# Nine full pieces of a head's probability blocks instead of twelve mixed ones

## The reference

```python
SEQ, MLA_HEADS, QK_HEAD, V_HEAD, Q_BLOCK = 1024, 16, 96, 64, 128
...
    def block(i):
        start = i * Q_BLOCK
        qb = lax.dynamic_slice_in_dim(q, start, Q_BLOCK, axis=1)
        s = jnp.einsum('bqhd,bkhd->bhqk', qb, k,
                       preferred_element_type=jnp.float32) * scale
        q_idx = start + jnp.arange(Q_BLOCK)
        s = jnp.where(k_idx[None, :] <= q_idx[:, None], s, -jnp.inf)
        p = jax.nn.softmax(s, axis=-1)
        return jnp.einsum('bhqk,bkhd->bqhd', p.astype(v.dtype), v)
...
    o = causal_attention(q, k, v)
    return x + (o * jax.nn.silu(z)) @ w_out
```

## Time and profile before

| what | us |
| --- | --- |
| median of three runs | 961.99 (960.85 to 962.02) |
| span of the profiled execution | 960.9 |
| TensorE matmul busy | 947.5 |
| VectorE busy | 812.9 |
| ScalarE busy | 575.2 |
| GpSimd busy | 353.1 |

### The profile page before, as it was taken

The page is one execution under the profiler, slowest core; times in us unless marked ns, Lnnn a source line. Parts: engine busy times, 40 slices in busy tenths (PEclk is TensorE's granted clock), DMA queues, the critical chain, the costliest instruction groups (busy, mean ns, idle before and its releaser), DMA issues.

```text
span 960.9 us, 17257 instructions
## 1 busy us (share of the span) xinstructions
PE 947.5 (99%) x6406; PEld 671.3 (70%) x6406; DVE 812.9 (85%) x1410; ACT 575.2 (60%) x1076; POOL 353.1 (37%) x393
## 2 busy tenths in 40 slices
PE   9999999999999999999999999998999999999998
PEld 8788544444688887644457999996788888887443
DVE  5798899899865579988887899998999999998763
ACT  6443544424434454454646888866899989997230
POOL 0002233222000002235412577875652478894220
PEclk9999999999999999999999999999999999999999
DMA  9320422111054422332123264566676775460231
GB/s 305 45 61 23 110 77 56 44 45 45 1 175 155 152 67 67 107 112 58 31 72 111 89 205 150 204 181 176 119 163 145 171 150 122 82 179 2 88 110 65
DMA packets 165347, 103.74 MB, mean 108 GB/s; under 512 B 75272, under 2 KB 149520, under 8 KB 165008
## 3 DMA queue, kind: packets, MB, share of 16 engines
q1 hardware_dynamic: 159216, 102.25, 38.0%
q10 hardware_dynamic: 6048, 0.39, 0.5%
HBM read 56.48 MB, written 29.36 MB: 89 GB/s over the span
## 4 chain that ended last, share of the span: by engine, by line
PE 72%; DVE 19%; POOL 3%; issue 3%; ACT 2%; DVEq 0%; POOLq 0%; ACTq 0%
PE banks L111 19%; PE banks L113 19%; PE banks L112 19%; PE banks L2728 7%; PE banks L2746 2%; PE banks L2748 2%; PE banks L2747 2%; DVE heads_y L2480 1%; POOL heads_prod L2616 1%; DVE heads_x L2476 1%; DVE heads_x L2475 1%; DVE front_lt L1223 1%; DVE heads_ss L2522 1%; PE banks L2756 1%; DVE front_l L1223 1%
## 5 line engine op out<-in xcount | busy, mean ns | idle before, releaser
L2497 DVE TENSOR_TENSOR heads_pt_lo<-banks,heads_pt_hi 128x512 f16<-128x512 f32 (+2 forms) x192 | 102.1, 554 | 10.8 <-ACT heads_pt_hi L2360 7.8
L2360 ACT ACTIVATE heads_pt_hi<-banks 128x512 f16<-128x512 f32 (+2 forms) x192 | 89.1, 487 | 9.1 <-PE banks L2728 8.9
L2748 PE MATMUL banks<-heads_v,heads_pt_lo 128*128 128x64 f16 x576 | 71.1, 194 | 0.0
L2747 PE MATMUL banks<-heads_v,heads_pt_hi 128*128 128x64 f16 x576 | 71.0, 194 | 0.0
L2489 DVE CUSTOM_DVE_ANT_0 heads_probs_big<-banks,heads_mask,score_scale 128x1024 f32<-128x1024 f32 (+1 forms) x64 | 68.6, 1072 | 2.9 <-PE banks L113 2.7
L2746 PE MATMUL banks<-heads_v,heads_pt_hi 128*128 128x64 f16 x576 | 70.9, 194 | 0.0
L2728 PE MATMUL banks<-ident,heads_probs_big 128*128 128x128 f32 x416 | 69.5, 281 | 1.2 <-ACT heads_probs_big L2351 1.1
L2351 ACT ACTIVATE heads_probs_big<-heads_probs_big,heads_neg_max 128x1024 f32<-128x1024 f32 (+1 forms) x64 | 63.4, 990 | 8.8 <-DVE heads_neg_max L2489 7.7
L111 PE MATMUL banks<-heads_k_t,heads_q_t 96*128 96x512 f16 (+2 forms) x192 | 63.0, 328 | 1.0 <-DVE heads_neg_max L2489 1.0
L111 PE MATMUL banks<-front_act_hi,front_w_hi 128*128 128x512 f32 x160 | 63.8, 399 | 0.0
L113 PE MATMUL banks<-front_act_hi,front_w_lo 128*128 128x512 f32 x160 | 62.4, 390 | 0.0
(11 more groups left out here) (489 smaller groups left out, 3114.5 us busy)
## 6 DMA issues: line engine op xcount, KB each, us to landing
qk_scratch<-heads_y SPq DMA_DIRECT2D x22, 512.0 KB, 3.7
front_x<-in_x_t SPq DMA_DIRECT2D x16, 512.0 KB, 5.3
front_raw<-in_w_in_ab SPq DMA_DIRECT2D x14, 512.0 KB, 5.1
qk_scratch<-heads_last_y SPq DMA_DIRECT2D x10, 512.0 KB, 3.8
front_w<-in_w_out_ab SPq DMA_DIRECT2D x8, 512.0 KB, 3.9
x_scratch<-front_x SPq DMA_DIRECT2D x8, 512.0 KB, 3.9
v_scratch<-heads_v SPq DMA_DIRECT2D x32, 128.0 KB, 3.0
heads_v_st<-v_scratch SPq DMA_DIRECT2D x8, 512.0 KB, 5.2
```

The source lines that it names most:

```text
L2360: nc.scalar.activation(pt_hi[:, q % PIECES, :width], t_ps[:, banks[("piece", n, k)] % 3, :width], ACT.Copy).then_inc(pt_high, 1)
L2497: nc.vector.tensor_tensor(pt_lo[:, q % PIECES, :width], t_ps[:, banks[("piece", n, k)] % 3, :width], pt_hi[:, q % PIECES, :width], ALU.sub ...
L2747: nc.tensor.matmul(o_part, pt_hi[:, q % PIECES, blk], v2[e][:, j, VH:], start=False, stop=False)
L2748: last = nc.tensor.matmul(o_part, pt_lo[:, q % PIECES, blk], v2[e][:, j, :VH], start=False, stop=(j == i))
```

## The change

The order of row tiles becomes 7, 3, 6, 0, 5, 1, 4, 2: tiles 0 and 2 change places. The rest of a wide tile is no longer a piece of its own; it shares a piece and a bank with the narrow tile behind it: tile 6's last three blocks with tile 0's one, tile 5's last two with tile 1's two, tile 4's last one with tile 2's three. Tile 7 has two full pieces and tile 3 one. So each position has one piece of four blocks, the first has two, and a head has nine. `PIECES_OF` writes that out. `high` and `low` always work on four blocks. Reciprocals, row maxima and the outputs of a head are kept by position instead of by row tile, so that the groups of four are contiguous; the output turn looks the position up.

```diff
-ORDER = (7, 3, 6, 2, 5, 1, 4, 0)
+ORDER = (7, 3, 6, 0, 5, 1, 4, 2)
...
-    def pieces(i):
-
-        return [range(b, min(b + 4, i + 1)) for b in range(0, i + 1, 4)]
...
+    PIECES_OF = (((0, range(0, 4)), (0, range(4, 8))), ((1, range(0, 4)),), ((2, range(0, 4)),),
+                 ((2, range(4, 7)), (3, range(0, 1))), ((4, range(0, 4)),), ((4, range(4, 6)), (5, range(0, 2))),
+                 ((6, range(0, 4)),), ((6, range(4, 5)), (7, range(0, 3))))
+
+    def pieces(n):
+
+        p, base = n % NT, n // NT * NT
+        if p == 0:
+            return [[(base, j) for j in blocks] for _, blocks in PIECES_OF[0]]
+        return [[(base + tile, j) for tile, blocks in PIECES_OF[p] for j in blocks]]
...
+    def turned_by(n):
+
+        last = n + 1 if n % NT in (2, 4, 6) else n
+        return piece_no(last, len(pieces(last)) - 1) + 1
...
-            nc.scalar.activation(pt_hi[:, q % PIECES, :width], t_ps[:, banks[("piece", n, k)] % 3, :width],
+            nc.scalar.activation(pt_hi[:, q % PIECES], t_ps[:, banks[("piece", n, k)] % 3],
                                  ACT.Copy).then_inc(pt_high, 1)
...
-            act.wait_ge(pv_done, piece_no(4 * g + 3, len(pieces(ORDER[(4 * g + 3) % NT])) - 1) + 1)
+            act.wait_ge(pv_done, piece_no(4 * g + 3, 0) + 1)
...
-                dve.wait_ge(pt_ready, piece_no(n - 4, len(pieces(tile_of(n - 4)[1])) - 1) + 1)
+                dve.wait_ge(pt_ready, turned_by(n - 4))
...
-            nc.vector.tensor_tensor(pt_lo[:, q % PIECES, :width], t_ps[:, banks[("piece", n, k)] % 3, :width],
-                                    pt_hi[:, q % PIECES, :width], ALU.subtract).then_inc(pt_low, 1)
+            nc.vector.tensor_tensor(pt_lo[:, q % PIECES], t_ps[:, banks[("piece", n, k)] % 3],
+                                    pt_hi[:, q % PIECES], ALU.subtract).then_inc(pt_low, 1)
...
-            nc.gpsimd.tensor_tensor(
-                pair_tiles(pair, g, e), o_raw[:, g % 2].rearrange("p (a b) d -> p a b d", a=2),
-                group_tiles(inv[:, h % 2], g).unsqueeze(3).to_broadcast([P, 2, 2, VH]),
-                ALU.mult).then_inc(o_scaled, 1)
+            nc.gpsimd.tensor_tensor(pair_tiles(pair, g, e), o_raw[:, g % 2],
+                                    group_tiles(inv[:, h % 2], g).unsqueeze(2).to_broadcast([P, 4, VH]),
+                                    ALU.mult).then_inc(o_scaled, 1)
...
-            for r, j in enumerate(pieces(tile_of(n)[1])[k]):
-                last = nc.tensor.transpose(t_ps[:, b, r * P:(r + 1) * P], probs(n, j * P, (j + 1) * P), ident[:])
+            for r, (m, j) in enumerate(pieces(n)[k]):
+                last = nc.tensor.transpose(t_ps[:, b, r * P:(r + 1) * P], probs(m, j * P, (j + 1) * P), ident[:])
...
-            o_part = o_ps[:, g % 2, o_slot(i), :VH]
-            for r, j in enumerate(pieces(i)[k]):
-                blk = slice(r * P, (r + 1) * P)
+            for r, (m, j) in enumerate(pieces(n)[k]):
+                i, blk, o_part = tile_of(m)[1], slice(r * P, (r + 1) * P), o_ps[:, g % 2, m % 4, :VH]
...
-                last = nc.tensor.transpose(t_ps[:, b, r * P:(r + 1) * P], o_pair[:, pair % 2, 4 * c + r, :], ident[:])
+                last = nc.tensor.transpose(t_ps[:, b, r * P:(r + 1) * P],
+                                           o_pair[:, pair % 2, ORDER.index(4 * c + r), :], ident[:])
```

More of the change, by code:

```diff
@@ L2175, in tile_of @@
         return divmod(n, NT)[0], ORDER[n % NT]
-    def pieces(i):
-        return [range(b, min(b + 4, i + 1)) for b in range(0, i + 1, 4)]
-    PER_HEAD = sum(len(pieces(i)) for i in range(NT))
+    PIECES_OF = (((0, range(0, 4)), (0, range(4, 8))), ((1, range(0, 4)),), ((2, range(0, 4)),),
[6 more added lines that the diff above has]
+        return [[(base + tile, j) for tile, blocks in PIECES_OF[p] for j in blocks]]
+    PER_HEAD = sum(len(pieces(p)) for p in range(NT))
     def piece_no(n, k):
         h, p = divmod(n, NT)
-        return PER_HEAD * h + sum(len(pieces(ORDER[x])) for x in range(p)) + k
+        return PER_HEAD * h + sum(len(pieces(x)) for x in range(p)) + k
+    def turned_by(n):
+        last = n + 1 if n % NT in (2, 4, 6) else n
+        return piece_no(last, len(pieces(last)) - 1) + 1
     def turn_step(pair, c):
@@ L2194, in heads_and_attention @@
         if n < N:
-            for k in range(len(pieces(tile_of(n)[1]))):
+            for k in range(len(pieces(n))):
                 banks[n_banks] = (pt_low, piece_no(n, k) + 1)
@@ L2224, in group_tiles @@
     def group_tiles(tile, g):
-        half = 1 if g % 2 == 0 else 0
-        return tile.rearrange("p (a c b) -> p a c b", a=2, c=2)[:, :, half, :]
+        return tile[:, g % 2 * 4:g % 2 * 4 + 4]
     def pair_tiles(pair, g, e):
[L2230 to L2235, removed]
+        return o_pair[:, pair % 2, g % 2 * 4:g % 2 * 4 + 4, e * VH:(e + 1) * VH]
     def sync(sp):
@@ L2350, in exponentials @@
             act.wait_ge(s_free, n + 1)
-            nc.scalar.activation(row, row, ACT.Exp, bias=neg_max[:, h % 2, i:i + 1], scale=-1.0,
-                                 accum_out=total[:, h % 2, i:i + 1]).then_inc(exp_done, 1)
+            at = n % NT
+            nc.scalar.activation(row, row, ACT.Exp, bias=neg_max[:, h % 2, at:at + 1], scale=-1.0,
+                                 accum_out=total[:, h % 2, at:at + 1]).then_inc(exp_done, 1)
         def high(n, k):
-            width = len(pieces(tile_of(n)[1])[k]) * P
             q = piece_no(n, k)
@@ L2487, in maxima @@
             if n >= 4:
-                dve.wait_ge(pt_ready, piece_no(n - 4, len(pieces(tile_of(n - 4)[1])) - 1) + 1)
+                dve.wait_ge(pt_ready, turned_by(n - 4))
             nc.vector.tensor_tensor_reduce(probs(n, 0, width), scores(i, 0, width), mask[:, S - width:],
                                            score_scale[:], 3e38, ALU.add, ALU.min,
-                                           neg_max[:, h % 2, i:i + 1]).then_inc(s_free, 1)
+                                           neg_max[:, h % 2, n % NT:n % NT + 1]).then_inc(s_free, 1)
         def low(n, k):
-            width = len(pieces(tile_of(n)[1])[k]) * P
             q = piece_no(n, k)
             dve.wait_ge(pt_high, q + 1)
-            nc.vector.tensor_tensor(pt_lo[:, q % PIECES, :width], t_ps[:, banks[("piece", n, k)] % 3, :width],
-                                    pt_hi[:, q % PIECES, :width], ALU.subtract).then_inc(pt_low, 1)
+            nc.vector.tensor_tensor(pt_lo[:, q % PIECES], t_ps[:, banks[("piece", n, k)] % 3],
+                                    pt_hi[:, q % PIECES], ALU.subtract).then_inc(pt_low, 1)
         def inverse(g):
@@ L2726, in transposes @@
                 pe.wait_ge(exp_done, n + 1)
-            for r, j in enumerate(pieces(tile_of(n)[1])[k]):
-                last = nc.tensor.transpose(t_ps[:, b, r * P:(r + 1) * P], probs(n, j * P, (j + 1) * P), ident[:])
+            for r, (m, j) in enumerate(pieces(n)[k]):
+                last = nc.tensor.transpose(t_ps[:, b, r * P:(r + 1) * P], probs(m, j * P, (j + 1) * P), ident[:])
             last.then_inc(pt_ready, 1)
         def product(n, k):
-            h, i = tile_of(n)
-            e, g = h % 2, n // 4
+            e, g = n // NT % 2, n // 4
             q = piece_no(n, k)
             if n % NT == 0 and k == 0:
-                pe.wait_ge(v_low, h + 1)
+                pe.wait_ge(v_low, n // NT + 1)
             if n % 4 == 0 and k == 0:
@@ L2801, in tensor @@
             old = n - BEHIND
-            new_pieces = len(pieces(tile_of(n)[1])) if n < N else 0
-            old_pieces = len(pieces(tile_of(old)[1])) if 0 <= old < N else 0
+            new_pieces = len(pieces(n)) if n < N else 0
+            old_pieces = len(pieces(old)) if 0 <= old < N else 0
             if n == N:
```

## The result

| | before | after |
| --- | --- | --- |
| median of five runs, us | 961.92 (960.85 to 962.02) | 965.13 (964.62 to 965.59) |
| span of the profiled execution | 960.9 | 963.8 |

The ratio is 1.0033, with an interval of 1.0023 to 1.0044: slower by a third of a per cent. The forecast was 965.3.

What follows compares the result with a forecast made beforehand. TensorE bounds the steady heads before; afterwards a ScalarE-VectorE loop was to. Steady part +2.7 us, end +0.6, first head 0: +3.3 on the 960.9 span, 964.2, and 1.1 more for the median: 965.3 us, 8-in-10 range 961.2 to 968.0.

Steps and rivals of the forecast that it cites:

- The loop as summed: Four turns a head of maxima, exponentials, copy, subtraction between VectorE and ScalarE: 13.50 us, against TensorE's 13.10.
- the rival that VectorE's total is the bound: VectorE's total work, not TensorE, bounds the kernel; less of it saves 7.2 us, giving 954.8; chance 0.04.
- The steady part: From tile 8's maxima to tile 126's: 200.87 us before, 203.54 forecast, so +2.7 us.
- The end: After tile 126's maxima: plain output products start at +3.83 us instead of +3.41, last products +0.17; +0.6 us in all.
- the first head: Stretch up to tile 8, paced by the last projections and a low-clock stretch: taken as 0, bounds -0.5 and +0.4 us.
- the two positions named: Positions 2 and 4 of a head, where TensorE was to wait for exponentials and for maxima.
- the third rival: TensorE's new waits, up to 0.4 us each, bring more stretches at half clock: 970 us; chance 0.07.
- edits with one answer: Tile order, semaphore waits, GpSimd's multiply, DMAs and piece slots: each costs 0, hidden by TensorE or the loop.
- a microsecond to spare: Before the change the loop took 12.04 us a head and hid under TensorE's 13.10.
- no longer on the path: In heads with an output turn, TensorE's eight transposes of that turn, 0.87 us, were to stop setting the pace.
- The gating: Wait of an output turn taken into the loop: 0.57 us, once in each of seven heads, 3.99 us.

Runs made afterwards that it cites:

- run 5: Changed kernel; from the third head on, copy and subtraction of odd positions' pieces treat two of four blocks, the rest left out: 961.13 us, ratio 0.9994.
- run 6: Changed kernel; from the third head on, copy and subtraction of even positions' last pieces treat two of four blocks, the rest left out: 964.20 us, ratio 1.0026.
- run 9: Changed kernel with a VectorE reciprocal of four columns added behind each odd position's subtraction: 968.18 us, ratio 1.0064.
- run 10: Changed kernel with a VectorE reciprocal of four columns added behind each even position's subtraction: 965.67 us, ratio 1.0039.
- run 11: Kernel before with the new order of tiles and bookkeeping by position, but its twelve pieces a head: 965.88 us, ratio 1.0038.
- run 2: Changed kernel with only the reciprocal of four row sums moved behind the next wide tile's maxima: 965.19 us, ratio 1.0030.
- run 12: Changed kernel with tile 6's rest of three blocks given its own piece and bank again, ten pieces a head: 963.72 us, ratio 1.0017.
- run 8: Kernel before with copy and subtraction of the wide tiles' rests, at even positions, taking all 512 columns: 966.81 us, ratio 1.0048.
- run 7: Kernel before with copy and subtraction of the narrow tiles' pieces, at odd positions, taking all 512 columns: 970.21 us, ratio 1.0089.
- run 1: Changed kernel with VectorE issuing odd positions' subtractions and the reciprocal behind the next wide tile's maxima: 979.69 us, ratio 1.0184.
- run 3: Changed kernel with a 32-column VectorE copy added behind each odd position's subtraction: 988.18 us, ratio 1.0273.
- run 4: Changed kernel with a 32-column VectorE copy added behind each even position's subtraction: 974.97 us, ratio 1.0137.

## Why the prediction was right, and where it was not

**The bound after.** The loop as summed is there: 13.41 us a head against 13.50. Each turn was read 0.02 or 0.03 too long, above all from maxima to exponentials (1.16 and not 1.19 at 896 columns, 0.89 and not 0.91 at 640). With runs 5, 6, 9 and 10 the loop is shown to set the pace of the heads without a turn, and the rival that VectorE's total is the bound is shown false. The Trainium skill (Perfetto Trace Analysis, Identifying the Most-Contended Engine) says to optimize first the engine of highest occupancy. The runs differ from it here: run 6 leaves VectorE busy 22.20 of 27 us and takes 964.2, run 5 leaves it 23.07 and takes 961.1.

**The sum.** The steady part was forecast at 203.54 and took 203.50, by errors that cancel, which is luck: 14 heads and most of a last one at 0.09 less are 1.3 us; the turn costs a head 0.71 (14.12 less 13.41) and not 0.57, seven times 0.14, 1.0 more (six heads and the last one, not seven before it); and the first of the 14 heads takes 13.71, 0.3 more (13.69 before). The end was forecast at 3.83 and 0.17 of products, and took 3.85 and 0.19. The 0.33 by which tile 8 comes earlier is not the first head's: its first maxima already come 0.46 earlier (658.37 against 658.83; the profiled runs here lie between 657.86 and 659.72), and it takes 0.13 longer, inside the bounds of that term.

**The waits.** In a head without a turn TensorE's distances exceed the usual ones by 0.53 us in all, 0.22 before. Of the 0.31 more, position 2's first transposes have 0.26 and position 4's 0.10, the two positions named; the rest of the head has a little less than before. The granted clock was 1.00, the upper of its two levels, from 676 to 885 us, so the third rival didn't come.

**The step that failed** in the account of what the change costs stands among the "edits with one answer": the order of tiles, at 0, "hidden by TensorE or the loop". Run 11 puts the order alone at 3.9 us over the kernel before (965.88 against 962.02 on the same chip). The sum still came out because the two losses don't add: in the heads without a turn, where the whole loop already sets the pace, the narrower chain of run 11 lies beside it (13.41 with both, 13.25 with the order alone). So the forecast named rightly what bounds the changed kernel's heads without a turn, but "the full pieces cost 3 us" doesn't follow. With the new order they cost nothing that can be told, 1.0033 (1.0023 to 1.0044) with them and 1.0038 (1.0025 to 1.0050) without: their heads without a turn are 0.16 longer, and the early ones with a turn 0.54 shorter. The prediction looked at the loop as one sum over a head, with a microsecond to spare before. It didn't ask whether each part of a head has its share of that; there the room was 0.2 us.

A second step failed in the heads with a turn: TensorE's transposes of the turn were taken to be "no longer on the path". The rows and four runs say that they are. The gating costs the loop its 0.57, as summed, and the copy that waits for TensorE 0.15 more. With the loop shortened by runs 2 and 12 these heads stay at 14.12; with the loop lengthened (run 9) or that copy halved (run 6) the turn costs 0.60.

No kernel with the whole computation was faster than the one before. **What is open**: the excess of run 8, the early heads with a turn of run 11, and run 2's time.

## What to carry to other kernels

Follow a piece of work round all engines that wait for each other in their written order, and sum the turns: an instruction on that loop costs each time what it delays the next start, and the same instruction beside it nothing, as long as it doesn't come to stand ahead of one on the loop (run 7). Make that sum for each part of a period too, against the work that covers it there, because moving cover from one position to another costs as much as lengthening the loop. Moving an instruction behind another one's wait closes a new loop (run 1), so name what stands in front of it before it moves.

## What the runs showed of the hardware that was not expected

A small copy on VectorE can last as long as the instruction that GpSimd is running. In run 3 the 34 copies that began with GpSimd idle took 172 ns in the median and 175 at most; the 30 that began while it was busy took 562 in the median and up to 2108. In run 4 it was 172 and 174 against 475 and 1651. The reciprocal of four columns, put in the same places in runs 9 and 10, kept a mean of 167 and 168 ns. The Trainium skill (SBUF — State Buffer, Who interferes with whom) has VectorE and GpSimd share a pair of SBUF ports that one instruction locks for its whole length, and counts the copy among the operations that can take the pair; the rows agree, with 172 ns against 2108. A copy put in as a measured load is therefore no constant load.
